# A fused two-block transformer kernel: heads scored in pairs, expert weights in shorter rows, and waits placed by tile

## The reference, cut to what matters

```
q_nope, q_rope = split((norm(c_q) @ w_uq) per head, 128 | 64)     # 8 heads
k_nope, v      = split((norm(c_kv) @ w_ukv) per head, 128 | 128)
k_rope         = rope(k_r)                                        # one for all heads
s   = (q_nope @ k_nope.T + rope(q_rope) @ k_rope.T) / sqrt(192), causal in chunks
y_a = softmax(s) @ v
x   = x + gate1 * ((g_m * (y_m @ w_branch_m) + g_a * (y_a @ w_branch_a)) @ w_out)
per expert e: y = (silu(xg @ w_gate[e]) * (xg @ w_up[e])) @ w_down[e]
out = rms_norm(x + gate2 * combined expert outputs)
```

## Time and profile before

| what | us |
|---|---|
| median of the runs | 1599.48 (1599.34 to 1601.65) |
| profiled execution | 1593.49 |
| its span | 1591.6 |
| second attention, first score to last values | 80 (1060.85 to 1141) |
| experts, first gate/up product to last down product | 253 (1309.76 to 1562.8) |

### The profile page before, as it was taken

One profiled execution on the slowest core, in us unless ns is written; L12 is line 12 of the kernel. 1 busy time (PEld: TensorE's weight loads), 2 busy tenths in 40 slices (PEclk: granted clock), 3 DMA queues, 4 the chain that ended last, 5 costly groups with the idle time before them and its releaser, 6 DMA issues.

```text
span 1591.6 us, 21261 instructions
## 1 busy us (share of the span) xinstructions
PE 1499.3 (94%) x8338; PEld 1187.4 (75%) x8338; DVE 783.7 (49%) x1494; ACT 455.0 (29%) x734; POOL 588.0 (37%) x486
## 2 busy tenths in 40 slices
PE   7999999999999999999999999999999989986885
PEld 6978887878888888877888988775688866644452
DVE  5565657377696863243714612356313354433334
ACT  4342334242231313252423241343313121100001
POOL 5551221435454545434543145420154412322222
PEclk9999999999999999999999999999999999999998
DMA  4250110335445442331222122210043689999996
GB/s 174 105 200 27 54 54 1 132 123 195 185 160 212 159 186 81 110 133 57 109 80 80 54 80 90 105 54 27 27 179 139 263 327 375 387 390 381 398 418 248
DMA packets 37348, 260.92 MB, mean 164 GB/s; under 512 B 6696, under 2 KB 7336, under 8 KB 13184
## 3 DMA queue, kind: packets, MB, share of 16 engines
q1 hardware_dynamic: 31488, 251.13, 41.3%
q0 software_dynamic: 5760, 8.41, 1.6%
HBM read 252.69 MB, written 17.30 MB: 170 GB/s over the span
## 4 chain that ended last, share of the span: by engine, by line
PE 83%; DVE 6%; issue 5%; ACT 2%; POOL 2%; DMA 1%; DVEq 0%; SPq 0%; ACTq 0%; POOLq 0%
PE G L2220 13%; PE G L2222 12%; PE G L2221 12%; PE SA L2808 4%; PE G L2808 4%; PE SA L2220 3%; PE SA L2222 3%; PE SA L2221 3%; PE PB L2222 3%; PE PB L2220 3%; PE PB L2221 3%; PE OB L2417 2%; POOL wl L771 1%; PE SA L2688 1%; PE G L2268 1%
## 5 line engine op out<-in xcount | busy, mean ns | idle before, releaser
L771 POOL TENSOR_TENSOR wl<-raw,wh 128x512 fp32r<-128x512 f32 x352 | 475.9, 1383 | 678.1 <-ACT wh L926 678.1
L926 ACT ACTIVATE wh<-raw 128x2048 fp32r<-128x2048 f32 x90 | 172.2, 1914 | 271.9 <-PE SA L2222 143.4
L2220 PE MATMUL G<-Hh,wh 128*128 128x512 f32 x544 | 216.3, 398 | 2.6 <-DVE arena L1618 1.4
L2222 PE MATMUL G<-Hh,wl 128*128 128x512 f32 x544 | 212.7, 391 | 0.0
L2221 PE MATMUL G<-Hl,wh 128*128 128x512 f32 x544 | 212.5, 391 | 0.0
L1695 DVE SCALAR_TENSOR_TENSOR arena<-arena,st 128x256 f32<-128x256 f32 x144 | 133.0, 924 | 5.1
L2220 PEld LDWEIGHTS G<-Hh,wh 128*128 128x128 f32 x544 | 102.5, 188 | 23.4 <-issue 2.2
L2222 PEld LDWEIGHTS G<-Hh,wl 128*128 128x128 f32 x544 | 102.4, 188 | 22.1
L2221 PEld LDWEIGHTS G<-Hl,wh 128*128 128x128 f32 x544 | 102.6, 189 | 19.4
L866 POOL DMA_INDIRECT raw<-xn_rows,arena x38 | 36.5, 960 | 120.8 <-PE G L2824 97.1
L2220 PE MATMUL G<-wh,Hh 128*128 128x256 f32 x256 | 77.6, 303 | 1.1 <-POOL wl L771 1.0
(11 more groups left out here) (536 smaller groups left out, 3084.0 us busy)
## 6 DMA issues: line engine op xcount, KB each, us to landing
raw<-in_pieces_dram SPq DMA_DIRECT2D x91, 1024.0 KB, 4.8
arena<-in_pieces_dram SPq DMA_DIRECT2D x24, 1024.0 KB, 4.8
arena<-in_wexp_dram SPq DMA_DIRECT2D x11, 2048.0 KB, 31.9
dn_w<-in_wexp_dram SPq DMA_DIRECT2D x18, 1024.0 KB, 36.9
arena<-in_wexp_dram SPq DMA_DIRECT2D x12, 1024.0 KB, 24.7
gu_y<-in_wexp_dram SPq DMA_DIRECT2D x6, 2048.0 KB, 29.2
gu_z<-in_wexp_dram SPq DMA_DIRECT2D x5, 2048.0 KB, 38.0
gu_h<-in_wexp_dram SPq DMA_DIRECT2D x4, 2048.0 KB, 33.7
```

The lines of the kernel that those rows point to most:

```text
L771: ins = pool.tensor_tensor(low_[:, part], whole[:, part], high[:, part], ALU.subtract)
L926: act.activation(split_pair(s)[0], wait_raw(act, sp_list[s]), ACT.Copy).then_inc(S("high_split"), 1)
L2220: pe.matmul(out, ah, bh, start=first, stop=False)
L2222: return pe.matmul(out, al, bh, start=False, stop=last)
```

## The change

- Heads are scored in pairs: at even steps the 128-row products of units t and t+1, then their two 64-row products. The score banks are now two pairs, SA and G[0:2] (SB). The turning of a unit is done two steps behind its score, the values three, the division four. The third score waits for the last value projection (va 7), whose bank it takes.
- yaT 0 to 5 all go to the third G bank, and each half is turned and taken in a step of its own; the first product of ga waits for all biased scores.
- h1 uses SA and PB; its first four tiles wait for wo 3, the last four for wo 15.
- Before qn the wait is for cT2 2; the wait for cT2 4 stands before the value projection.
- Gate and up weights of an expert come in two transfers of 8 KB rows, where it was one of 16 KB rows; who waits for them counts twice as far.
- Eight fill-in products ahead of the first rows of the experts, where it was five ahead and three behind.

```diff
-ATTENTION_BANKS = ("qr", "down", "om", "vm", "wout")
+ATTENTION_BANKS = ("qr", "down", "om", "vm", "wout", "h1")
...
+        elif what == "yaT" and i < 6:
+            b = GRING - 1
...
+        SB = (SA, G[0:2])
...
-                sp.dma_start(wgu[b % NSLOT], wexp[b, :, 0:2 * PIECE]).then_inc(S(f"gu_loaded{b % NSLOT}"), 16)
+                for j in range(2):
+                    part = slice(j * PIECE, (j + 1) * PIECE)
+                    sp.dma_start(wgu[b % NSLOT][:, part], wexp[b, :, part]).then_inc(S(f"gu_loaded{b % NSLOT}"), 16)
...
-                if t >= 11 and (t - 11) % 8 == 0 and t < len(aunits):
-                    attended_high((t - 11) // 8)
+                if t >= 12 and (t - 12) % 8 in (0, 2) and t < len(aunits):
+                    attended_high((t - 12) // 8, [(t - 12) % 8 // 2])
...
-                dve.tensor_tensor_reduce(SP3[:, u % 2, 0:nk], SA[u % 2][:, 0:nk], chunk[:, T - nk:T], -ASCALE, 3e38,
+                dve.tensor_tensor_reduce(SP3[:, u % 2, 0:nk], SB[u // 2 % 2][u % 2][:, 0:nk], chunk[:, T - nk:T], -ASCALE, 3e38,
...
-                if h == 0 and q:
-                    wait_group(dve, "yaT", 2 * q - 1)
+                if h % 4 == 0 and q:
+                    wait_group(dve, "yaT", 2 * q - 2 + h // 4)
...
-            for t in range(len(aunits) + 5):
-                if 0 <= t - 3 < len(aunits):
-                    aout(t - 3)
+            for t in range(len(aunits) + 7):
+                if 0 <= t - 4 < len(aunits):
+                    aout(t - 4)
                 if t < len(aunits):
                     abiased(t)
-                if 0 <= t - 1 < len(aunits):
-                    acopied(t - 1)
-                if t >= 11 and (t - 11) % 8 < 2:
-                    q, i = divmod(t - 11, 8)
+                if 0 <= t - 2 < len(aunits):
+                    acopied(t - 2)
+                if t >= 12 and (t - 12) % 8 in (0, 2):
+                    q, i = (t - 12) // 8, (t - 12) % 8 // 2
...
-            wait_freed(pe, "wo", 15)
             for f in range(KT):
+                wait_freed(pe, "wo", 15 if f >= KT // 2 else 3)
                 transposes("h1", f, [Xv[:, t, f * P:(f + 1) * P] for t in range(NT)])
...
-            wait_freed(pe, "cT2", 4)
+            wait_freed(pe, "cT2", 2)
...
+            wait_freed(pe, "cT2", 4)
             for i in range(6):
                 value_rows(i, wv)
...
-                r = slice(64 * (h % 2), 64 * (h % 2) + 64)
-                pe.wait_ge(S("score_biased"), A0 + u - 1)
-                pe.matmul(SA[u % 2][:, 0:nk], qn[:, h, q * P:(q + 1) * P], kn[:, h, 0:nk], start=True, stop=False)
-                pe.matmul(SA[u % 2][:, 0:nk], qrT[r, h // 2, q * P:(q + 1) * P], krT[r, 0:nk], start=False, stop=True).then_inc(S("scores_ready"), 1)
+                banks = SB[u // 2 % 2]
+                if u == 2:
+                    wait_freed(pe, "va", 7)
+                pe.wait_ge(S("score_biased"), A0 + max(u - 2, 0))
+                for n in range(2):
+                    pe.matmul(banks[n][:, 0:nk], qn[:, h + n, q * P:(q + 1) * P], kn[:, h + n, 0:nk], start=True, stop=False)
+                for n in range(2):
+                    r = slice(64 * n, 64 * n + 64)
+                    pe.matmul(banks[n][:, 0:nk], qrT[r, h // 2, q * P:(q + 1) * P], krT[r, 0:nk], start=False, stop=True).then_inc(S("scores_ready"), 1)
...
-            for t in range(len(aunits) + 2):
-                if t < len(aunits):
+            for t in range(len(aunits) + 3):
+                if t < len(aunits) and t % 2 == 0:
                     ascores(t)
-                if 0 <= t - 1 < len(aunits):
-                    aturned(t - 1)
-                if t >= 10 and (t - 10) % 8 == 0:
-                    attended_turned((t - 10) // 8)
-                if t == len(aunits) + 1:
+                if 0 <= t - 2 < len(aunits):
+                    aturned(t - 2)
+                if t >= 11 and (t - 11) % 8 in (0, 2) and t < len(aunits):
+                    attended_turned((t - 11) // 8, [(t - 11) % 8 // 2])
+                if t == len(aunits) + 2:
+                    pe.wait_ge(S("score_biased"), A0 + len(aunits))
                     one_feature("ga", ("ga", 0), 0, 0, range(4))
-                if 0 <= t - 2 < len(aunits):
-                    avalues(t - 2)
+                if 0 <= t - 3 < len(aunits):
+                    avalues(t - 3)
...
-            hold(5)
+            hold(8)
             rows_of(0)
             rows_of(1)
-            hold(3)
...
-                pe.wait_ge(S(f"gu_loaded{b % NSLOT}"), slot_count(b))
+                pe.wait_ge(S(f"gu_loaded{b % NSLOT}"), 2 * slot_count(b))
```

More of the change, by code:

```diff
@@ L728, in _ @@
                         sp.wait_ge(S("up_ready"), NE - WS + WS * i + v + 1)
-                        sp.dma_start(wgu[s].rearrange("p (o n) -> p o n", o=1),
-                                     wexp[bass.ds(e, 1), :, 0:2 * PIECE].rearrange("o p n -> p o n")).then_inc(S(f"gu_loaded{s}"), 16)
+                        for j in range(2):
+                            part = slice(j * PIECE, (j + 1) * PIECE)
+                            sp.dma_start(wgu[s][:, part].rearrange("p (o n) -> p o n", o=1),
+                                         wexp[bass.ds(e, 1), :, part].rearrange("o p n -> p o n")).then_inc(S(f"gu_loaded{s}"), 16)
                         sp.wait_ge(S("y_ready"), NE - WS + WS * i + v + 1)
@@ L1233, in aunit, with attended_high @@
                                accum_out=rsum2[:, (q % 2) * 8 + h:(q % 2) * 8 + h + 1]).then_inc(S("probs_ready"), 1)
-            def attended_high(q):
-                for i in range(2):
+            def attended_high(q, halves=range(2)):
+                for i in halves:
                     b = wait_group(act, "yaT", 2 * q + i)
@@ L2708, in avalues, with attended_turned @@
                 ins.then_inc(S("values_summed"), 1)
-            def attended_turned(q):
+            def attended_turned(q, halves=range(2)):
                 pe.wait_ge(S("a_out"), 8 * q + 8)
-                for i in range(2):
+                for i in halves:
                     transposes("yaT", 2 * q + i, [ya[:, (4 * i + f) * P:(4 * i + f + 1) * P] for f in range(4)])
-            for t in range(len(aunits) + 2):
-                if t < len(aunits):
+            for t in range(len(aunits) + 3):
+                if t < len(aunits) and t % 2 == 0:
                     ascores(t)
-                if 0 <= t - 1 < len(aunits):
-                    aturned(t - 1)
-                if t >= 10 and (t - 10) % 8 == 0:
-                    attended_turned((t - 10) // 8)
-                if t == len(aunits) + 1:
+                if 0 <= t - 2 < len(aunits):
[4 more added lines that the diff above has]
+                    pe.wait_ge(S("score_biased"), A0 + len(aunits))
                     one_feature("ga", ("ga", 0), 0, 0, range(4))
-                if 0 <= t - 2 < len(aunits):
-                    avalues(t - 2)
+                if 0 <= t - 3 < len(aunits):
+                    avalues(t - 3)
             one_feature("ga", ("ga", 0), 0, 0, range(4, KT))
@@ L2883, in _ @@
                         pe.wait_ge(S("xgT_ready"), b + 1)
-                        pe.wait_ge(S(f"gu_loaded{s}"), before + 16 * i + 16)
+                        pe.wait_ge(S(f"gu_loaded{s}"), 2 * before + 32 * i + 32)
                         pe.wait_ge(S("act_whole"), b - 1)
```

## The result

| | before | changed |
|---|---|---|
| median of the runs, us | 1598.21 (1594.56 to 1601.65, 11 runs) | 1604.76 (1602.31 to 1610.77, 11 runs) |
| profiled execution (span), us | 1593.49 (1591.6) | 1606.17 (1604.3) |
| second attention, first scores to last values, us | 80.1 | 91.8 |

The ratio is 1.0044, with an interval of 1.0034 to 1.0053: the changed kernel is slower by 6.6 us. The two profiled executions are 12.7 us apart, because that of before lies 4.7 us under its own median and that of after 1.4 over. Part of it is half-clock spells elsewhere in the program: from 739 us on the trace of after has one, in which products of 512 columns start 0.43 us apart where the trace of before has 0.23, and which costs 3.2 us. They come and go from execution to execution.

The account below looks back on a forecast made before the run. TensorE was taken to bound the second attention, weight transfers the experts' last part. Attention +8, clock +2, h1 -2.2, cT2 -1.6, fill-in products and 8 KB rows 0: +6.2 on the 1599.48 us median, 1605.7 us, range 1592 to 1614.

Parts of the forecast that it names:

- The pairs give 12.8 us: Second attention: 64-row products of two heads overlap, saving 0.48 to 1.12 us a pair, 12.8 us in all.
- Rival (2): Second attention: the 64-row products don't overlap; 8.5 us more, 1614 us; chance 0.06.
- The pairs take, by the single output bank: Second attention: values wait for the previous unit's division, 1.0 to 0.7 us a pair; net 1.7 us longer.
- rival (1): Second attention: the pairs' gain shows in full, division never late; 1583 us, about 1595 with half the stalls; chance 0.22.
- The turned outputs: Second attention, yaT halves in separate steps: two steps in eight stall 1.5 us longer; 6.1 us more over three sets.
- The clock: Second attention: stalls lower TensorE's granted clock to 0.95, costing 2 us, range 0 to 6.
- Rival (3): Second attention: the clock falls to 0.89 throughout; 4 us more, 1610 us; chance 0.12.
- h1 and cT2: Waits around h1's turnings and behind cT2's, ahead of qn: earlier starts gain 2.2 and 1.6 us.
- Fill-in products: Ahead of the experts: first expert could start 1.6 us earlier, but transfers are the bound, so 0 at the end.
- 8 KB rows: Experts' gate and up transfers: same bytes in twice the issues, 0 us, kept at -4 to +4.
- rival (4): Experts' last stage: transfers 2% faster or slower with 8 KB rows; 1601 or 1610.5 us; chance 0.12, half each way.
- Rival (5): Experts' end: late transfers set the end, so the attention's delay vanishes; 1599.5 us; chance 0.04.

Follow-up runs that it names:

- the attention alone: The kernel before with only the second attention changed: ratio 1.0068, median 1608.28 us, attention 92.0 us.
- the third slot: Changed kernel with a second output bank, the second turned half four steps behind the first, and a third place for the probabilities: ratio 0.9898, median 1581.28 us.
- the pairs in turn: Changed kernel with second output bank and later second half, each head's 64-row product behind its own 128-row product: ratios 1.0122 and 1.0069.
- the filled stalls: Changed kernel with fill-in products in every second unit of the attention, three where a half is turned: ratio 1.0124, median 1616.08 us.
- two output banks: Changed kernel with values of even and odd units in separate banks and three score banks instead of four: ratio 0.9990, attention 81.3 us.
- the attention undone: Changed kernel with its second attention as it was before, all other edits kept: ratio 0.9977, median 1593.54 us.

## Why the prediction was right

1605.7 us was forecast and 1604.76 measured, by the mechanism named; as differences, 6.2 us forecast and 6.6 measured. Step by step:

- **What bounds the kernel.** Held: what the attention lost or won arrived at the end, 10.7 us over before with the attention alone and 15 under with the third slot (11.6 by the attention, 3.8 by the two waits), and the stretch behind the attention has 439 to 443 us in every trace. Two kernels, the pairs in turn and the filled stalls, lost more in their medians than their one traced attention explains.
- **The pairs give 12.8 us.** Held: the scores of a pair of q=3 take 1.14 us less where 1.12 was forecast, and putting the products in turn costs 13.9. TensorE's whole work at full clock fell by less, from 78.7 us to 67.5 (two output banks), 11 us: values behind a wait take 0.74 us to the next start where the same take 0.67 without one, and turning the outputs takes 0.49 us a half where both together took 0.88. Rival (2), no overlap, falls.
- **The pairs take, by the single output bank.** Held: forecast 1.0, 0.9, 0.8, 0.7 us of wait a pair for q=0 to 3, measured 0.92 to 1.05 (q=0), 0.98 (q=1), 0.92 (q=2), 0.85 (q=3). The second output bank took the wait away and with the rest of that chain 6.9 us (88.2 to 81.3). That is also why rival (1) failed: the gain is there, and the division is what kept it back.
- **The turned outputs.** Held in cause, a little high in size. I had 2.4 us for both long waits of a set; measured 1.8 to 2.0 for the first and 2.25 to 2.43 for the second. And I let the one bank of all yaT groups off as hidden in the stall, where it makes the first of these waits: two steps more between the halves gave 7.3 us.
- **Sum of the attention.** Forecast +8 by the order, measured +8.1. That it fits to 0.1 us is luck: 66 us of work and 22 of stall were forecast, and 67.5 and 20.8 came, two errors of 1.5 and 1.2 us that cancel.
- **The clock.** Right in sign, too small: forecast +2 (0 to 6), measured 3.6 in the profiled execution. Six traces have this attention unchanged: five lie between 91.4 and 92.0 us, one has 93.5. Rival (3), a clock of 0.89 throughout, didn't come: it was 0.96. The half-clock spell of the earlier trace rows that the prediction lays to gaps of a few tenths stands behind a wait of 1.14 us at 262 us (clock 0.82 and 0.75 in the two stretches of 4 us from 260, 1.00 in the two behind).
- **h1 and cT2.** -2.2 and -1.6 forecast, 2.2 and 1.5 in the trace, 4.0 together by the run with the attention undone.
- **Fill-in products.** 0 forecast at the end for 1.6 us at the first expert; 1.8 there and none at the end.
- **8 KB rows.** 0 forecast; between 0 and -3, so rival (4) is left as a possible gain of its lower half only. Rival (5), that the late transfers swallow the attention's delay, falls by the run of the attention alone. The two stretches of the earlier trace rows were misread: in the first, 132 packets of 8 KB or more carry 1.32 MB, 10 KB each on average, so it is not 8 KB rows only, and in the second 256 such packets carry 3.3 MB, 12.8 KB each, so it is not nearly all 16 KB rows. Two mixtures at the same rate still speak for no difference, but less strongly. The Trainium skill, "DMA: Bandwidth & Descriptors" (Anatomy of one DMA), gives its fixed cost of about 2 us for transfers that GpSimd issues, and these are issued by SyncE; no run here prices one alone.

The terms of the trace sum to 8.1 + 3.6 - 2.2 - 1.5 = 8.0 us, and the runs have 6.6. The clock is the likeliest place for the difference, as the term that varies between executions; that is not shown.

What the prediction did not see is how near the gain was. It weighed that the pairs' 12.8 us show or do not show, and not which two small obstacles stood between: an output bank and two steps of distance. With both removed the attention is 6 us shorter than before, with a third slot 11.6.

## What to carry to other kernels

When work is taken from the engine that bounds a loop, write down the chain through the other engines for one round of it and compare it with what is left to do on the first engine: a gain ends where a buffer with one place makes that chain the longer one. Count the places of each buffer between two engines (scores, probabilities, turned probabilities, outputs): a change that draws instructions together in twos can need one place more in some of them. Here a second output bank gave 6.9 us and a third slot for the probabilities 5.6, while the scores did as well with three banks as with four. Two uses of one bank want as many steps between them as the engines behind it need; here moving one by two steps gave 7.3 us and cost nothing that was seen.

## What the hardware showed

- Two float32 products of 64 rows each, on rows 0 to 63 and 64 to 127 and in two banks, start 0.01 us apart and take 1.06 us for 512 columns, the time of one; with a 128-row product between them they take their full time each (1.05 us). The order of these products is worth 13.9 us in an attention of 74, the switches between 128 and 64 rows included.
- TensorE's clock fell to 1.2 GHz for 22 us (granted 0.51) while it was busy for 21.1 of them, in one of two executions (on two chips) with the same products and the same wait of 0.59 us ahead. So the wait ahead of it does not decide alone, and one profiled execution prices the clock of a stretch only for itself.
- The kernel with its pairs in turn and the one with its waits filled had executions 19 and 14 us apart; those of every other kernel stayed within 12 us. Why is open: both keep TensorE busier in that attention than the changed kernel does (81.9 and 78.7 us against 71.0), but so does the kernel before (78.7).
